# Block one in another order: u, z, gates, a, glu, wb, wa, wo, with x's split rows rewritten normed behind u

## The reference

```
h = rmsnorm(x, norm_g);  proj = h @ w_in                       # 2048 -> 14336
v, bg, cg, za, u, zb, ga, gb = split(proj)                     # 4 x 2048, 2 x 1024, 2 x 2048
ya = (bg * causal_conv3(cg * v)) * silu(za);  ya = ya @ w_out_a
yb = gelu(s5_scan(u, ...));  yb = yb * sigmoid(yb @ w_glu + b_glu)
yb = (yb * silu(zb)) @ w_out_b
m = sigmoid(ga) * ya + sigmoid(gb) * yb
x1 = rmsnorm(x + m @ w_o, final_g)
```

## Time and profile before

| what | value |
|---|---|
| runs | 2502.61, 2502.80, 2502.87 us |
| span of the profiled execution (first to last instruction) | 2501.5 us |
| TensorE busy | 2491.3 us, 11932 matmuls |
| VectorE busy | 1660.5 us |
| ScalarE busy | 848.8 us |
| GpSimd busy | 383.1 us |
| mean DMA rate | 141 GB/s |

### The profile page before, as it was taken

One profiled execution on the slowest core, in us unless ns is written; L12 is line 12 of the kernel. 1 busy time (PEld: TensorE's weight loads), 2 busy tenths in 40 slices (PEclk: granted clock), 3 DMA queues, 4 the chain that ended last, 5 costly groups with the idle time before them and its releaser, 6 DMA issues.

```text
span 2501.5 us, 30081 instructions
## 1 busy us (share of the span) xinstructions
PE 2491.3 (100%) x11932; PEld 2157.3 (86%) x11932; DVE 1660.5 (66%) x2218; ACT 848.8 (34%) x1153; POOL 383.1 (15%) x286
## 2 busy tenths in 40 slices
PE   9999999999999999999999999999999999999998
PEld 8888888888888888888888888878888888888888
DVE  7789888998988776555554885657566564244434
ACT  5222222222222322223322333333565664333432
POOL 0045343444443431000000000000000000000001
PEclk9999999999999999999999999999999999999999
DMA  5333333333333433667666676624322222322333
GB/s 202 103 121 111 119 120 115 122 117 111 119 111 128 136 123 126 218 222 253 204 209 212 211 249 211 218 91 152 101 85 85 85 77 93 118 96 92 124 127 126
DMA packets 117963, 353.07 MB, mean 141 GB/s; under 512 B 15424, under 2 KB 18752, under 8 KB 117824
## 3 DMA queue, kind: packets, MB, share of 16 engines
q1 hardware_dynamic: 117824, 351.16, 42.4%
HBM read 321.68 MB, written 23.07 MB: 138 GB/s over the span
## 4 chain that ended last, share of the span: by engine, by line
PE 99%; DVE 0%; DMA 0%; SPq 0%; ACT 0%; issue 0%; DVEq 0%
PE bank L552 29%; PE bank L553 29%; PE bank L554 29%; PE bank L752 2%; PE bank L753 2%; PE bank L751 2%; PE bank L805 1%; PE bank L795 1%; PE bank L615 1%; PE bank L603 1%; PE bank L715 1%; PE bank L788 0%; PE bank L786 0%; DMA W<-in_w 0%; PE bank L847 0%; PE bank L767 0%
## 5 line engine op out<-in xcount | busy, mean ns | idle before, releaser
L1273 DVE TENSOR_TENSOR WL<-W,WH 128x1024 fp32r<-128x1024 f32 (+1 forms) x452 | 600.9, 1333 | 441.1 <-ACT WH L924 440.1
L924 ACT ACTIVATE WH<-W 128x1024 fp32r<-128x1024 f32 (+1 forms) x452 | 473.8, 1050 | 900.5 <-PE bank L554 653.4
L552 PE MATMUL bank<-hH,WH 128*128 128x512 f32 x1792 | 681.3, 380 | 0.8 <-DVE hL L1569 0.3
L554 PE MATMUL bank<-hH,WL 128*128 128x512 f32 x1792 | 679.3, 379 | 0.0
L553 PE MATMUL bank<-hL,WH 128*128 128x512 f32 x1792 | 679.3, 379 | 0.0
L552 PEld LDWEIGHTS bank<-hH,WH 128*128 128x128 f32 x1792 | 338.7, 189 | 58.2 <-issue 5.0
L554 PEld LDWEIGHTS bank<-hH,WL 128*128 128x128 f32 x1792 | 338.7, 189 | 48.1
L553 PEld LDWEIGHTS bank<-hL,WH 128*128 128x128 f32 x1792 | 338.9, 189 | 47.2
L552 PE MATMUL bank<-h2H,WH 128*128 128x512 f32 x624 | 239.4, 384 | 0.0
L553 PE MATMUL bank<-h2L,WH 128*128 128x512 f32 x624 | 236.6, 379 | 0.0
L554 PE MATMUL bank<-h2H,WL 128*128 128x512 f32 x624 | 236.6, 379 | 0.0
(11 more groups left out here) (308 smaller groups left out, 3608.9 us busy)
## 6 DMA issues: line engine op xcount, KB each, us to landing
W<-in_w SPq DMA_DIRECT2D x332, 512.0 KB, 3.7
W<-in_ada SPq DMA_DIRECT2D x96, 512.0 KB, 4.3
W<-in_wa SPq DMA_DIRECT2D x32, 512.0 KB, 3.9
W<-in_wo SPq DMA_DIRECT2D x32, 512.0 KB, 3.8
W<-in_wvv SPq DMA_DIRECT2D x32, 512.0 KB, 3.7
W<-in_wb SPq DMA_DIRECT2D x16, 512.0 KB, 3.7
URAW<-U SPq DMA_DIRECT2D x96, 64.0 KB, 3.1
scr_am<-SO SPq DMA_DIRECT2D x16, 256.0 KB, 2.0
```

The source lines that it names most:

```text
L552: e.matmul(o, wh, xh, start=first, stop=False)
L554: return e.matmul(o, wl, xh, start=False, stop=last)
L924: e.activation(chunk_parts(n)[0][:, c], W[:, i % NW, c], ACT.Copy).then_inc(sem["hi"], 1)
L1273: e.tensor_tensor(wl[:, c], W[:, plan.item_of[n] % NW, c], wh[:, c].bitcast(F32), ALU.subtract).then_inc(sem["lo_v"], 1)
```

## The change

The order of the first block becomes u, zb, gates, a, glu, wb, wa, wo. With it:

- Behind u, hH and hL are written a second time, now normed. GpSimd multiplies the sixteen rows XS by RSA in place (signal xn), ScalarE writes hH again and VectorE hL (function normed on both). Rows 0 to 7 come behind u's last instructions, rows 8 to 15 behind the first unit of z, in each engine's program. TensorE waits for each row in the first z projection (n_ready). u itself is still made from the rows that are not normed.
- z, gates and a need no factor any more: ScalarE reads z's and the gates' banks with Silu or Sigmoid straight into SO, and za's with Silu into T. VectorE's scalings, RSS and GpSimd's product in a are gone.
- The state-space tiles are spread from unit 28 to the end of a's c = 5 (SSM_C, unit 143).
- The a products are fetched back one by one at positions AM_AT of glu and wb into SO (signal am_in) and split there. gelu and the split of yb move into the last c of a. wb's result times its gate is kept (MB), wa's is added to it.
- The modulation chunks begin with glu, twelve at one per two units, then 52 at one per unit; the last 32 go beside the second block's v and its u and gate projections, summed in a second accumulator ACC[1].
- The small parameter products use T instead of V; buffers move accordingly.

```diff
-SSM_GATES = 13
+SSM_C = 5
-A_GATES = 16
+AM_AT = {1: 0, 3: 1, 5: 2, 7: 3, 8: 4, 9: 5, 10: 6, 12: 7, 13: 8, 14: 9, 16: 10, 17: 11, 18: 12, 20: 13, 21: 14,
+         22: 15}
...
+        for m in range(8):
+            self.proj("zb", [w1[72 + m, c] for c in range(2)])
+        for m in range(32):
+            self.proj("gate", [w1[80 + m, c] for c in range(2)])
         for c in range(16):
             for part in (0, 2, 1, 3):
                 self.proj("a", [w1[16 * part + c, kc] for kc in range(2)])
...
+        for i in range(12):
+            self.ada += [ada[i:i + 1], []]
+        self.ada += [[x] for x in ada[12:64]]
...
+        for i in range(0, 32, 16):
+            self.ada += [[], []] if i == 0 else []
+            self.ada += [ada[64 + i:66 + i]] + [[x] for x in ada[66 + i:80 + i]]
...
-            self.reduce_at[n + (6 if i == 63 else 4)] = i // 16
+            self.reduce_at[n + 4] = i // 16
...
-    tiles_to = plan.last(gate_p[SSM_GATES - 1])
+    tiles_to = plan.last(a_p[4 * SSM_C + 3])
...
         # TensorE
-        for p in a_p + spill_p:
-            project(p, xh, xl, beside=ssm_until)
+        def n_ready(k):
+            e.wait_ge(*nth("xl", 16 + k))
+
+        for i, p in enumerate(spill_p + a_p):
+            project(p, xh, xl, n_ready if i == 0 else None, beside=ssm_until)
...
         # ScalarE
+        def normed(k):
+            e.wait_ge(sem["used"], plan.last(u_p[7]) + k // 8)
+            e.wait_ge(*nth("xn", k))
+            e.activation(hH[:, k, :], XS[:, k, :], ACT.Identity, scale=col["g1"][:, k:k + 1]).then_inc(sem["xh"], 1)
+
+        for k in range(8):
+            normed(k)
+        for s, p in enumerate(spill_p):
+            ssm_until(unit())
+            if s == 0:
+                for k in range(8, 16):
+                    normed(k)
+            ssm_until(unit())
+            projected(p)
+            if s >= 2:
+                e.wait_ge(spilled[s % 2], 16 * (s // 2))
+            e.activation(halves(SO[:, s % 2, :]), tokens(bank[bank_of[p]][:, :]),
+                         ACT.Silu if s < 8 else ACT.Sigmoid).then_inc(sem["sp_a"], 1)
...
         # VectorE, behind keep_u(7)
+        def normed(k):
+            e.wait_ge(*nth("xh", 16 + k))
+            e.scalar_tensor_tensor(out=hL[:, k, :], in0=XS[:, k, :], scalar=col["g1"][:, k:k + 1],
+                                   in1=hH[:, k, :].bitcast(F32), op0=ALU.mult,
+                                   op1=ALU.subtract).then_inc(sem["xl"], 1)
+
+        for k in range(8):
+            normed(k)
+        for s in range(len(spill_p)):
+            ssm_until(unit())
+            if s == 0:
+                for k in range(8, 16):
+                    normed(k)
+            ssm_until(unit())
...
         # VectorE, in a
-                    e.tensor_tensor(cv, cv, RSS, ALU.mult).then_inc(sem["a_v"], 1)
...
-                    e.tensor_tensor(halves(T[:, 2, :]), tokens(bank[bank_of[p]][:, :]), halves(RSA[:, :]),
-                                    ALU.mult).then_inc(sem["a_v"], 1)
...
-            e.tensor_tensor(halves(SO[:, s % 2, :]), tokens(bank[bank_of[p]][:, :]), halves(RSA[:, :]),
-                            ALU.mult).then_inc(sem["sp_v"], 1)
...
+        def low_a(at):
+            k = AM_AT.get(at)
+            if k is not None:
+                e.wait_ge(*nth("al_a", k))
+                e.tensor_tensor(AL[:, k, :], SO[:, k % 2, :], AH[:, k, :].bitcast(F32),
+                                ALU.subtract).then_inc(sem["al_v"], 1)
...
         # GpSimd
+        e.wait_ge(*nth("rsa", 0))
+        for k in range(16):
+            e.wait_ge(*nth("xsq", k))
+            e.wait_ge(*nth("xl", k))
+            e.tensor_tensor(XS[:, k, :], XS[:, k, :], RSA[:, :], ALU.mult).then_inc(sem["xn"], 1)
```

More of the change, by code:

```diff
@@ L81, in __init__ @@
                 self.proj("a", [w1[16 * part + c, kc] for kc in range(2)])
[L82 to L89, removed]
+        ada = [t["ada"][part, k] for part in ADA_ORDER for k in range(16)]
+        for i in range(12):
+            self.ada += [ada[i:i + 1], []]
+        self.ada += [[x] for x in ada[12:64]]
         for m in range(8):
@@ L93, in __init__ @@
             self.proj("wb", [t["wb"][m, 0]])
+        for m in range(16):
+            self.proj("wa", [t["wa"][m, c] for c in range(2)])
         for m in range(16):
@@ L118, in chunk @@
         if self.ada:
-            src = self.ada.pop(0)
-            if src is not None:
+            for src in self.ada.pop(0):
                 self.ada_chunk(src)
@@ L158, in program @@
     si_in = [nc.alloc_semaphore(f"si_in{i}") for i in range(2)]
+    am_in = [nc.alloc_semaphore(f"am_in{i}") for i in range(2)]
     x1_out = [nc.alloc_semaphore(f"x1_out{i}") for i in range(2)]
@@ L305, in program @@
     for i, p in enumerate(spill_p):
-        read[p] = [nth("sp_v", i)]
+        read[p] = [nth("sp_a", i)]
     for c in range(16):
@@ L444, in sp_program, with load_a @@
             e.dma_start(scratch["am"][c], SO[:, c % 2, :]).then_inc(spilled[c % 2], 16)
[L445 to L457, removed]
         e.wait_ge(spilled[0], 16 * 28)
         e.wait_ge(spilled[1], 16 * 28)
-        for d in range(16):
-            e.wait_ge(*(nth("ma", d - 2) if d >= 2 else nth("al_v", 14 + d)))
+        def load_a(at):
+            k = AM_AT.get(at)
+            if k is not None:
+                if k >= 2:
+                    e.wait_ge(*nth("al_v", k - 2))
+                e.dma_start(SO[:, k % 2, :], scratch["am"][k]).then_inc(am_in[k % 2], 16)
+        for g in range(8):
+            if g >= 2:
+                e.wait_ge(*nth("g_v", g - 2, 2))
+            load(scratch["zb"][g])
+            load_a(g)
+            unit()
+        for d in range(16):
+            e.wait_ge(*(nth("b_v", d - 2) if d >= 2 else nth("g_v", 6 + d, 2)))
+            load(scratch["gb"][d])
+            load_a(8 + d)
+            unit()
+        for d in range(16):
+            e.wait_ge(*(nth("m", d - 2, 1) if d >= 2 else nth("b_v", 14 + d)))
             load(scratch["ga"][d])
             unit()
[L464 to L471, removed]
             unit()
@@ L1008, in act_program @@
                     ssm_until(unit())
+                if c == 15:
+                    for k in range(4 * (i % 2), 4 * (i % 2) + 4):
+                        (gelu_y if i < 2 else high_y)(k)
                 if i == 0:
@@ L1013, in act_program, with high_a @@
                     e.activation(halves(T[:, 0, :]), tokens(bank[bank_of[p]][:, :]), ACT.Copy).then_inc(sem["a_a"], 1)
[L1014 to L1035, removed]
-                i = d - 1
-                e.wait_ge(sem["yb_a"], i + 1)
-                e.activation(ybH[:, i, :], U[:, i, :], ACT.Copy).then_inc(sem["yb_a"], 1)
-            unit()
+                if i == 3:
+                    projected(p)
+                    if c > 0:
+                        e.wait_ge(*nth("a_v", c - 1, 6))
+                    e.activation(halves(T[:, 2, :]), tokens(bank[bank_of[p]][:, :]), ACT.Silu).then_inc(sem["a_a"], 1)
+        def high_a(at):
+            k = AM_AT.get(at)
+            if k is not None:
+                e.wait_ge(am_in[k % 2], 16 * (k // 2 + 1))
+                e.activation(AH[:, k, :], SO[:, k % 2, :], ACT.Copy).then_inc(sem["al_a"], 1)
         for g, p in enumerate(wg_p):
@@ L1611, in dve_program @@
                     ssm_until(unit())
+                if c == 15 and i >= 2:
+                    for k in range(4 * (i - 2), 4 * (i - 2) + 4):
+                        low_y(k)
                 if i == 1:
@@ L1687, in dve_program @@
         for d, p in enumerate(wb_p):
+            unit()
+            projected(p)
+            si = gate_in(at_load)
+            at_load += 1
+            e.tensor_tensor(halves(MB[:, d, :]), tokens(bank[bank_of[p]][:, :]), halves(si),
+                            ALU.mult).then_inc(sem["b_v"], 1)
+            low_a(8 + d)
+        for d, p in enumerate(wa_p):
+            unit()
             unit()
```

175 lines of the change are left out of this document (81 added, 94 removed).

## The result

The new kernel takes 2524.98 us (median of four runs, 2523.87 to 2526.33), the kernel before 2502.84 (four runs): 22.1 us more, ratio 1.0089, 95% interval 1.0074 to 1.0103. The forecast was 2512.5 with a range to 2522. The sign was right, and so were the handover's queue and the load of VectorE in the packing. The size was not, and for GpSimd's multiplications and for the clock the mechanism was not either.

A forecast was written before the change was run, and what follows sets the result against it. TensorE was taken to bound the kernel, with next to no gaps. Handover 7.0 us (GpSimd's 1 included) plus packing 3, all else 0, made 10 us on 2501.5 + 1.3: 2512.8, written 2512.5, range 2506.5 to 2522.

The forecast's parts named there:

- The sign: Whole kernel: slower by over 5 us, chance 0.82; within 5 us 0.15; faster 0.03.
- GpSimd's multiplications: Sixteen multiplications of x by 1/rms beside VectorE: lateness reaching unit 15, bounds 0 and about 4 us, taken as 1 us.
- The frame: Whole kernel: TensorE at its floor, same products reordered, 0 us; the question is whether the new order opens gaps.
- The scalings' 53 us: VectorE loses 53 us of scalings, all beside a TensorE that never waited for it: 0 us on the path.
- The handover: Behind u: TensorE waits 3.1 and 2.7 us for rewritten rows queued on VectorE, plus pace 0.1 each: 6.0 us.
- The packing: Tiles in units 28 to 143 fill VectorE in a's first six c, 43.6 us in 43.5: 3 us, bounds 0 to 12.
- rival 3: At the handover's two 3 us waits the clock falls to 1.2 GHz: 3 to 5 us more, 2516; chance 0.09.
- The modulation chunks: Moved to glu and later, the last 32 beside the second block's half-idle VectorE: 0 us, bounds 0 and 1.
- Rival 4: Not slower: VectorE gets through early at the handover, which costs 4.3 us at most, 2507 or less; chance 0.15.
- Rival 2: The tiles' packing dominates: VectorE falls behind in all six c of a, 7 + 12 = 19 us, 2522; chance 0.13.

The follow-up runs named there:

- experiment 3: New kernel with VectorE's rewritten rows put ahead of keep_u(7) and parameter steps at the handover, steps of units 15 to 26 one unit later: 2517.3 us.
- experiment 2: New kernel with GpSimd's sixteen multiplications of x by 1/rms cut to two columns each: 2519.5 us.
- experiment 8: Kernel before the change with GpSimd's sixteen multiplications alone added, CB's memset moved before them, two later steps waiting for the last: 2506.3 us.
- experiment 1: New kernel with the state-space tiles spread wider, to c = 10 of a instead of c = 5: 2515.9 us.
- experiment 6: Kernel before the change, its own order, with the state-space tiles packed to end at unit 143: 2584.4 us.
- experiment 7: New kernel with the state-space read-out one phase later in TensorE's queue: 2523.3 us.
- experiment 5: New kernel with GpSimd's multiplications whole but spaced, two per unit of TensorE from unit 8 on: 2523.2 us.
- Experiment 10: New kernel with VectorE's parameter steps kept off the multiplications, tiles from unit 33 to c = 13, VectorE's rows in front at the handover: 2505.0 us.
- experiment 4: New kernel with eleven small identity products on TensorE before each of its waits for rows 0 and 8: 2522.4 us.

## Why the prediction was wrong

**The frame held.** The same products in the same number, nothing to win, and the question which gaps open. The scalings' 53 us of VectorE were worth nothing, as said.

**The handover (6.0 us forecast and 1 for GpSimd, 7.9 measured).** The queue read off rows 6 gave 3.1 and 2.7 us and a pace of 0.66; the trace has 3.2, 2.9 and 0.66, and experiment 3 takes both waits away. What was missing is the 1.8 us of half clock; the 1 us put in for GpSimd's lateness at this place did not come, as VectorE and TensorE both arrive 4.6 us late.

**GpSimd's multiplications (the step that failed by mechanism; that 1 us forecast, 4.5 measured).** The step took the size of the mutual blocking from a long instruction, 0.36 us on 1.23, and looked for its effect in unit 15, with VectorE's room averaged over 53 to 84 us. The cost came from the small ones: each of twelve parameter instructions of 0.18 to 0.2 us waited out most of a multiplication of 1.3 us (21.36 for sixteen) and took 1.2, 12 us more together in a stretch where the old VectorE had 8 to 9 us idle, and what met it was the low half of chunk 12, at 74 us. Experiments 2 and 8 show it from both sides (5.5 less, 3.4 more). The Trainium skill's rule (SBUF — State Buffer, "Who interferes with whom") was the better guide: the loser waits for the whole instruction, and by the same section tensor_scalar can take part too. The trace agrees, with lines 1386 and 1388 at 1224 and 1222 ns.

**The packing (3 us forecast, 8.5 measured).** The load was right: 43.6 us of work in 43.5 forecast, and VectorE is 98% busy there. Mis-sized was the reserve. I looked for it only at the low halves and charged 0.5 us a c; TensorE's queue is in order, and the read-out, which needs the last phase of the tile before, has less. One meeting cost 4.9 us and 2.4 of half clock. Experiments 1 (9.1 us back) and 6 (81 us more in the old order) confirm the cause, and 7 that the place is only where it is met.

**The clock (left to rival 3 at 0.09; 5.9 us, counted in the sums above).** The row that I read, four us idle at full clock at the tail, was taken as evidence against. Of the four waits of 2.8 to 4.9 us three had a stretch at 0.50 at their end or behind them. Not every such wait has: the one at 98 us had not, and the profiles of experiments 1 and 7 have a gap of 3.03 us at unit 12 with the clock full behind it. So the price of a wait here is its length and up to 2.4 us more, 3 in experiment 5. The runs of the new kernel spread over 2.5 us, where the old kernel's first four lie within 0.3; that the clock makes this spread is likely, not shown. The Trainium skill's warning (TensorE: Matmul & The Clock Gate, "HAM oscillation — how this bites in real kernels") applied.

**The modulation chunks (0 us forecast, at most 1; 2.1 measured).** VectorE is half idle beside the second block's v and gates, as the prediction says, but a chunk stood directly in front of a low half. Experiment 10, where little else is left, has the same loss. No run tests the chunks alone. The share of busy time said nothing about the order in the queue.

Rival 4 (not slower) fell with the handover. Rival 2's 2522 was nearest in number by luck: its 12 us were 2 in each of six c, where the trace has 1.2 and 7.3 in two of them, and it had nothing for unit 12 or the clock.

## What to carry to other kernels

Where TensorE has no idle time, an edit can only cost, and moved work is priced in the in-order queue of the engine that feeds it: what stands in front, and which of TensorE's waits has the least reserve. GpSimd instructions in a row beside a chain of small VectorE instructions cost that chain up to one GpSimd length per link (here 1.2 us for 0.19); spacing them does not help where VectorE has no room left. Keep the chain out of their way. To a wait of TensorE as long as those here (2.8 to 7.4 us) add what the clock may take behind it, 0 to 3 us here. A low share of busy time does not make a place free: look at what will stand in front of the next operand.

## What the runs showed of the hardware

A VectorE tensor_scalar or scalar_tensor_tensor on 128x32 took 1.2 us beside GpSimd's 128x512 multiplications and 0.18 to 0.20 us without. The wait of TensorE at unit 12, 2.6 us by its own entry (2.99 to 3.04 from product to product), was followed by half clock in four kernels' profiles (the new one, experiments 3, 4 and 8) and not in two (1 and 7). Eleven small identity products in front of each of the handover's two waits kept it at full there.
